# Moving a fourth expert from the loop into the fixed group, with the third weight matrix read in 8 KB runs

## The reference, cut to what matters

```python
def swiglu(h, w1, w3, w2):
    return (jax.nn.silu(h @ w1) * (h @ w3)) @ w2
...
    logits = (xt @ w_router).astype(jnp.float32)
    top_logits, top_idx = lax.top_k(logits, TOP_K)
    gates = jax.nn.softmax(top_logits, axis=-1)
...
    def expert_block(args):
        x_blk, e = args
        return swiglu(x_blk, w1[e], w3[e], w2[e])
```

## Time and profile before

| | |
|---|---|
| median of 3 runs | 1801.97 us (1798.7 to 1804.3) |
| the profiled execution | 1791.78 us, span 1790.1 us |
| up to the experts | 706 us |
| job 0 | 706 to 842 us |
| group, 168 slots | 842 to 1399 us |
| loop, three passes of 42 slots | 1399 to 1772.7 us |
| PE busy over the span | 94% |

### The profile page before, as it was taken

How to read it: one execution, slowest core, us unless ns; L and a number is a source line. 1 busy time by engine, 2 the same in 40 slices (tenths; PEclk the granted TensorE clock), 3 DMA queues, 4 the chain that set the end, 5 groups by cost and what they waited for, 6 DMA issues and landing times.

```text
span 1790.1 us, 23711 instructions
## 1 busy us (share of the span) xinstructions
PE 1686.4 (94%) x8929; PEld 1396.9 (78%) x8929; DVE 1400.4 (78%) x1439; ACT 1011.1 (56%) x953; POOL 65.5 (4%) x85
## 2 busy tenths in 40 slices
PE   5999979999999898999999999999999899999996
PEld 5988869999898877778777777776777688788875
DVE  4887777888788765997688777877887788888877
ACT  1544533333454445675666666666666667767664
POOL 1000100000100011000000000000000010010120
PEclk9998999999999898999999999999999999999999
DMA  9455657888545564997898898988899899999993
GB/s 309 151 174 158 232 165 232 271 285 272 189 158 171 188 213 166 357 356 269 314 338 322 296 333 314 341 319 313 326 327 348 298 367 375 360 378 362 359 390 154
DMA packets 270282, 503.62 MB, mean 281 GB/s; under 512 B 12630, under 2 KB 113256, under 8 KB 270184
## 3 DMA queue, kind: packets, MB, share of 16 engines
q1 hardware_dynamic: 262736, 489.72, 78.0%
q0 software_dynamic: 3056, 11.01, 1.8%
q10 hardware_dynamic: 4392, 1.57, 0.4%
HBM read 493.36 MB, written 8.91 MB: 281 GB/s over the span
## 4 chain that ended last, share of the span: by engine, by line
issue 42%; PE 40%; DVE 9%; ACT 4%; POOL 2%; DVEq 1%; ACTq 1%; POOLq 1%; DMA 0%
PE ps L1883 10%; PE ps L1885 9%; PE ps L1884 9%; DVE lo_ring L1789 5%; PE ps L2212 4%; PE ps L2211 4%; DVE lo_ring L1535 2%; ACT stage_hi L1151 2%; PE ps L2338 2%; ACT stage_hi L1085 1%; DVE xn L1824 1%; POOL rstd L814 1%; PE ps L2175 1%; POOL y_back L878 0%; POOL rstd L805 0%
## 5 line engine op out<-in xcount | busy, mean ns | idle before, releaser
L1789 DVE TENSOR_TENSOR lo_ring<-weight_ring,stage_hi 128x2048 fp32r<-128x2048 f32 x168 | 379.1, 2288 | 88.8 <-ACT stage_hi L1151 88.3
L1535 DVE TENSOR_TENSOR lo_ring<-weight_ring,stage_hi 128x2048 fp32r<-128x2048 f32 x168 | 378.2, 2288 | 61.7 <-ACT stage_hi L1085 61.1
L1085 ACT CAST stage_hi<-weight_ring 128x2048 fp32r<-128x2048 f32 x168 | 314.2, 1912 | 61.8 <-DMA weight_ring<-in_moe_w_dram 56.6
L1151 ACT CAST stage_hi<-weight_ring 128x2048 fp32r<-128x2048 f32 x168 | 314.4, 1911 | 5.7 <-DMA weight_ring<-in_moe_w_dram 5.7
L1883 PE MATMUL ps<-h_hi,stage_hi 128*128 128x256 f32 x800 | 233.2, 292 | 8.1 <-DVE h_lo L1248 6.3
L1883 PE MATMUL ps<-stage_hi,xe_hi 128*128 128x512 f32 x560 | 227.3, 406 | 10.2 <-DVE lo_ring L1535 8.8
L1285 DVE TENSOR_TENSOR lo_ring<-weight_ring,stage_hi 128x2048 fp32r<-128x2048 f32 x81 | 184.9, 2292 | 64.7 <-ACT stage_hi L950 57.3
L1884 PE MATMUL ps<-h_lo,stage_hi 128*128 128x256 f32 x800 | 229.6, 287 | 0.0
L1885 PE MATMUL ps<-h_hi,lo_ring 128*128 128x256 f32 x800 | 229.4, 287 | 0.0
L1884 PE MATMUL ps<-lo_ring,xe_hi 128*128 128x512 f32 x560 | 221.3, 395 | 0.0
L1885 PE MATMUL ps<-stage_hi,xe_lo 128*128 128x512 f32 x560 | 221.2, 395 | 0.0
(11 more groups left out here) (379 smaller groups left out, 2565.5 us busy)
## 6 DMA issues: line engine op xcount, KB each, us to landing
weight_ring<-in_moe_w_dram SPq DMA_DIRECT2D x336, 1024.0 KB, 6.9
weight_ring<-in_w_mod_dram SPq DMA_DIRECT2D x48, 1024.0 KB, 6.1
weight_ring<-in_w_in_dram SPq DMA_DIRECT2D x36, 1024.0 KB, 5.5
weight_ring<-in_ffn_w_dram SPq DMA_DIRECT2D x33, 1024.0 KB, 5.7
weight_ring<-in_w_out_dram SPq DMA_DIRECT2D x12, 1024.0 KB, 5.0
moe_rows<-y_moe POOLq DMA_DIRECT2D x5, 512.0 KB, 4.8
moe_rows<-y_e POOLq DMA_DIRECT2D x4, 512.0 KB, 8.2
x_tok<-in_x_dram SPq DMA_DIRECT2D x1, 1024.0 KB, 10.9
```

Source lines behind the costliest of these rows:

```text
L1085: nc.scalar.copy(jst_hi[i % JSTAGES][:], ring[:, n % RING, :]).then_inc(hi_ready, 1)
L1151: nc.scalar.copy(jst_hi[g % JSTAGES][:], ring[:, n % RING, :]).then_inc(hi_ready, 1)
L1535: nc.vector.tensor_tensor(ring_lo[:, n % RING, :], ring[:, n % RING, :], raw(jst_hi[i % JSTAGES][:]), ALU.subtract).then_inc(lo_ready, 1)
L1789: nc.vector.tensor_tensor(ring_lo[:, n % RING, :], ring[:, n % RING, :], raw(jst_hi[g % JSTAGES][:]), ALU.subtract).then_inc(lo_ready, 1)
```

## The change

The fourth smallest expert goes from the loop into the group: the loop has two passes, the group 210 slots. `behind` gets two runs of six S slots in each middle chunk, and four such runs in the last one. The columns, row places and step lists follow. The ACT wait for the last `sum` is gone; the last S expert ends before the last B slot (half 1 of w2), which takes its two blocks in the other order; the number of passes is read before the group on ACT, PE and DVE; and in a loop pass ACT copies `y_e` after four casts and after PE's first slot, no longer after three casts. In w2 the partition p now holds rows 4p to 4p+3 of a chunk, so that a transfer has runs of 8 KB in place of two of 4 KB for each partition. To match, every transposition of an activation (job 0, group and loop) takes every fourth column of its input.

```diff
-EXTRA = 3
+EXTRA = 4
...
-NSMALL = 3
-LOOP_MIN, LOOP_MAX = 4, 4 + EXTRA
+NSMALL = 4
+NOTHER = NE - 2 - NSMALL
+LOOP_MIN, LOOP_MAX = 1 + NOTHER, 1 + NOTHER + EXTRA
...
-        behind = [3, 1 if ch == 0 else 3, 1, 5, 3, 3] if ch < NCH - 1 else [3, 3, 6, 6, 0, 2]
+        behind = [3, 1 if ch == 0 else 3, 6, 6, 3, 3] if ch < NCH - 1 else [6, 6, 6, 6, 2, 0]
...
+def lag(c):
+
+    return 1 if c == LAST_C else 2
+
+
+def half_order(ch):
+
+    return (1, 0) if ch == NCH - 1 else (0, 1)
...
-                    (s_at(PLACES_C), ("places", 0)), (AT["B", "w2", NCH - 1, 1], ("next", 0)),
-                    (sum_at(2), ("sum", 2)))
+                    (s_at(PLACES_C), ("places", 0)), (sum_at(NSMALL - 1), ("next", 0)),
+                    (G_SLOTS, ("sum", NSMALL - 1)))
...
-    w2_v = moe_w2[0].rearrange("e (t p) n -> e p t n", p=P)
+
+    w2_v = moe_w2[0].rearrange("e (c p t) n -> e p c (t n)", p=P, t=4)
...
-            return w2_v[bass.ds(e, 1), :, ch * 4 + half * 2:ch * 4 + half * 2 + 2, :].rearrange("e p t n -> (e p) t n")
+            return w2_v[bass.ds(e, 1), :, ch:ch + 1, half * 2 * D:(half + 1) * 2 * D].rearrange("e p c n -> (e p) c n")
...
-                    act.wait_ge(st_used, ahead(job) + ND)
+                split(3)
+                if not first:
+
+                    act.wait_ge(st_used, ahead(job) + (ND + 1))
                     act.wait_ge(y_free, job + 1)
                     nc.scalar.copy(y_e[:], pair(YB)).then_inc(ye_out, 1)
-                split(3)
...
-            act.wait_ge(ssum_done, NSMALL)
...
-                        last = nc.tensor.transpose(ps[:, TPB, k * P:(k + 1) * P], m_act[:, ch % 2, k * P:(k + 1) * P], ident[:])
+                        last = nc.tensor.transpose(ps[:, TPB, k * P:(k + 1) * P], m_act[:, ch % 2, :].rearrange("p (n t) -> p t n", t=4)[:, k, :], ident[:])
...
-                    for t in range(TT):
+                    for t in half_order(c) if h else range(TT):
...
-                                last = mm(ps[:, SUP, at:at + SMALL], part[:, k * P:(k + 1) * P], fold[:], start=True, stop=True)
+                                last = mm(ps[:, SUP, at:at + SMALL], part.rearrange("p (n t) -> p t n", t=4)[:, k, :], fold[:], start=True, stop=True)
```

More of the change, by code:

```diff
@@ L180, in sum_at @@
     return AT["S", "w2", NCH * j + NCH - 1, 1]
-PLACES_C = 16
+def lag(c):
+    return 1 if c == LAST_C else 2
+def half_order(ch):
+    return (1, 0) if ch == NCH - 1 else (0, 1)
+PLACES_C = 22
 CS, BS = range(NSMALL * NCH), range(NCH)
-GROUP_PE = steps_at(*[(s_at(c), ("sT", c)) for c in CS], *[(s_at(NCH * j - 1), ("rows", j)) for j in (1, 2)],
-                    *[(b_at(ch), ("bT", ch)) for ch in BS], *[(sum_at(j) + 3, ("sum", j)) for j in range(2)],
-                    (s_at(PLACES_C), ("places", 0)), (AT["B", "w2", NCH - 1, 1], ("next", 0)),
-                    (sum_at(2), ("sum", 2)))
+GROUP_PE = steps_at(*[(s_at(c), ("sT", c)) for c in CS], *[(s_at(NCH * j - 1), ("rows", j)) for j in range(1, NSMALL)],
+                    *[(b_at(ch), ("bT", ch)) for ch in BS], *[(sum_at(j) + 3, ("sum", j)) for j in range(NSMALL - 1)],
+                    (s_at(PLACES_C), ("places", 0)), (sum_at(NSMALL - 1), ("next", 0)),
+                    (G_SLOTS, ("sum", NSMALL - 1)))
@@ L189 @@
 GROUP_ACT = steps_at((2, ("y0", 0)),
                      *[(AT["S", "w1", c, 1] + 2, ("s1", c)) for c in CS], *[(AT["S", "w3", c, 1] + 2, ("s3", c)) for c in CS],
-                     *[(s_at(c) + 2, ("silu", c)) for c in CS], *[(s_at(NCH * j - 1) + 2, ("rows", j)) for j in (1, 2)],
-                     *[(s_at(c) + 3, ("hi", c)) for c in CS],
+                     *[(s_at(c) + lag(c), ("silu", c)) for c in CS], *[(s_at(NCH * j - 1) + 2, ("rows", j)) for j in range(1, NSMALL)],
+                     *[(s_at(c) + lag(c) + 1, ("hi", c)) for c in CS],
@@ L193 @@
                      *[(AT["B", "w1", ch, 1] + 2, ("bsilu", ch)) for ch in BS], *[(b_at(ch) + 2, ("bhi", ch)) for ch in BS],
[L194 to L197, removed]
+                     *[(sum_at(j) + 2, ("raw", j)) for j in range(NSMALL - 1)],
@@ L198 @@
+                     *[(sum_at(j) + 5, ("sum", j)) for j in range(NSMALL - 1)],
+                     (G_SLOTS, ("next", 0)), (G_SLOTS, ("raw", NSMALL - 1)))
+GROUP_DVE = steps_at(*[(s_at(c) + lag(c), ("act", c)) for c in CS], *[(s_at(NCH * j - 1) + 2, ("rows", j)) for j in range(1, NSMALL)],
+                     *[(s_at(c) + lag(c) + 1, ("lo", c)) for c in CS],
                      *[(AT["B", "w3", ch, 1] + 2, ("bact", ch)) for ch in BS], *[(b_at(ch) + 2, ("blo", ch)) for ch in BS],
@@ L518, in build @@
         posj, mskj, gatej = (m(n, [P, TT, NCOL + 1]) for n in ("posj", "mskj", "gatej"))
[L519 removed]
+        pose, gate = (m(n, [P, TT, NE]) for n in ("pose", "gate"))
+        gmsk = drow
         selT = m("selT", [P, TT, P])
         cnts, over, ranki, rank, far = (m(n, [P, NE]) for n in ("cnts", "over", "ranki", "rank", "far"))
[L522 to L523 removed]
+        key, place, cap, few, base, step1, step_few, step7 = (m(n, [P, NE]) for n in (
+            "key", "place", "cap", "few", "base", "step1", "step_few", "step7"))
         shift = m("shift", [P, NCOL])
@@ L826, in _ @@
                     serve_blocks(l, ("post_mix", "post_ffn")[i])
-            cleared = [(k * P, P) for k in [0] + list(range(COL_LOOP + 3, NCOL + 1))]
-            cleared += [((COL_SMALL + j + 1) * P + SMALL, P - SMALL) for j in range(2)]
+            cleared = [(k * P, P) for k in [0] + list(range(COL_LOOP + NOTHER, NCOL + 1))]
+            cleared += [((COL_SMALL + j + 1) * P + SMALL, P - SMALL) for j in range(NSMALL - 1)]
             pool.wait_ge(y_zero, 1)
@@ L846, in _ @@
             nc.gpsimd.drain().then_inc(y_free, 1)
-            for j in range(2):
+            for j in range(NSMALL - 1):
                 row = (COL_SMALL + j + 1) * P
@@ L1814, in _ @@
                     elif step == "bsum":
-                        for t in range(TT):
-                            if t == 0:
+                        for n_half, t in enumerate(half_order(c)):
+                            if n_half == 0:
                                 dve.wait_ge(b_done, c + 1)
@@ L2302, in _ @@
                                                (wh[:, k, s], wl[:, k, s]), kk == 0, kk == 3)
-                        if h and t == 0:
+                        if h and t == half_order(c)[0]:
                             last.then_inc(b_done, 1)
```

36 lines of the change are left out of this document (18 added, 18 removed).

## The result

The changed kernel takes **1861.43 us** (median of 4 runs, 1858.69 to 1868.34) against 1802.93 for the kernel before on the same chip (4 runs): ratio 1.0339 [1.0322, 1.0355], **slower**. I had forecast 1787, faster. The profiled execution took 1861.65.

What follows compares the result with a forecast made beforehand. PE was taken to bound the kernel, with the DMA engines nearly full. The terms -122.6 + 95.0 + 16 - 4 gave -15.6, say -15 us, from the 1801.97 median to 1787 us; range 1770 to 1845.

Steps and rivals of the forecast that it cites:

- every fourth column: Fold and transposition loads stepping 16 bytes: taken as nothing; doubled loads bounded at 47.5 us for folds, 13.9 for transpositions.
- Rival 1: Fold and transposition loads by fourths are slow: full price +61 us, 1848 us, also visible in job 0; chance 0.27.
- the fold block: Sign in the group's folds: 16 take 1.7 us if skipping loads cost nothing, about 3.4 if they are slow.
- What leaves: Loop: the middle one of three passes goes, -122.6 us.
- What comes in: Group: a fourth small expert's matmuls, folds, row gather and final sum, +95.0 us.
- Waits of the new order: Group: PE waits in added runs of six S slots, behind ACT's copy and cast and DVE's subtraction, +16 us.
- The passage: Group to loop: PE starts the loop 4.9 us after its last group matmul, 2.9 less; with clock effect -4 us.
- Runs of 8 KB: w2 transfers: half as many packets, hidden under PE's matmuls, worth nothing; up to the +16 of waits if slots come early.
- Rivals 2 and 3: Group held by its slots, 3.32 us each: 1815 us, chance 0.11; earlier slots close waits: 1770 to 1759 us, chance 0.12.
- the sum: Whole kernel: -122.6 + 95.0 + 16 - 4 = -15.6 us.

Runs made afterwards that it cites:

- four only: Changed kernel with contiguous transpositions and the old w2 transfer runs, keeping the fourth small expert, order and passage; 1794.91 us, ratio 0.9942 to the kernel before.
- the wait back: The four only version with ACT's old wait for the last sum restored in front of the loop; 1793.72 us, ratio 0.996 to the kernel before.
- the contiguous version: Changed kernel keeping its 8 KB layout, but reading contiguous columns, so w2 meets wrong columns; 1796.65 us, ratio 0.9966 to the kernel before.
- pairs: Changed kernel with two w2 rows per partition, still 8 KB runs, transpositions taking every second column (8 bytes); 1796.73 us, ratio 0.9958 to the kernel before.
- fourths only: Kernel before with only the 8 KB w2 transfers and every-fourth-column transpositions added, three small experts; 1852.76 us, ratio 1.0282 to the kernel before.
- half by fourths: Changed kernel with the first 8 folds of each block stepping by four columns, the other 8 contiguous; 1819.55 us, ratio 1.0081 to the kernel before.
- four steps: Changed kernel with contiguous transpositions and folds stepping 4, 8, 12 or 16 bytes by chunk, taking wrong columns; 1821.54 us, one run.

## Why the prediction was wrong

**The step that failed** is the one headed *every fourth column*: "I take nothing, by the nearest row". The row was a moving operand that comes in at 0.45 ns a column, and I concluded that a load at 0.9 was not at the limit of the memory. That row reads *contiguous* columns, so it says nothing of a read that skips, and the forecast had said itself that no row shows one. The folds measured +51.2 us, a little above the upper bound of 47.5, since a fold by fourths takes 0.221 us and not twice 0.106. The transpositions, bounded at 13.9, cost some 1 us: a block of eight takes 0.87 us where it takes 0.79 with four only (and the earlier trace rows shows 0.79 for eight others, of the gathered rows), although their loads grew from 141 to 207 ns. Their pace is not that of their loads, contrary to what I took. Rival 1 (chance 0.27, 1848 us) was the right mechanism, with the fold block as the sign that was named for it. That its 1848 lies near 1861 is in part luck: it holds 13.9 for transpositions that cost some 1, and nothing for the clock. Job 0, where it was to show too, has transpositions but no folds and is only 0.8 us longer.

**What no case held** is the clock. Against four only, 20.3 us of excess and 4.3 in the gathers, 24.6 in all, come from stretches at 1.2 GHz behind the slower blocks; without them the time would be some 1837, inside the range. I had priced the doubling of a load as added time only, and not asked what PE's doing less work in that time does to the clock; the first pass in the earlier trace rows, with 0.98 behind an idle stretch, was a hint that the clock answers to that.

**What held.**
- *What leaves*: -122.6 for a pass; the loop is 124.4 shorter, the difference being its faster first pass (124.73 against 125.40) and last pass (124.56 against 125.70).
- *What comes in*: +95.0; 77.8, 12.0, 3.5 and 1.9 make 95.2.
- *Waits of the new order*: +16; the waits before the S matmuls rose from 13.9 to 30.2, +16.3, the idle time in all by 17.4. That those of 1.12 us hang on ACT's copy of the w1 product is shown by moving the copy; for those of 1.3 us it is argued only, since they stayed.
- *The passage*: 4.9 us forecast from the last group matmul to the loop, 4.9 measured (the row at 1588.16 plus one distance, to 1593.27), against 7.8 before. Putting the wait back brings 1.7 us of it in the trace; the remainder goes with the last slot being a B slot, which was not tried alone.
- *Runs of 8 KB*: nothing, as forecast, by the contiguous version. Rivals 2 and 3 are out with it: the group of 42 more slots is 673 us at contiguous reads, not 557 + 139 - 3 = 693, and the waits did not close.

Left alone, the fourth expert and the passage give -8.7 us where the sum said -15.6. In the traces its expert part is 5.6 shorter: the loop gives 122.1, and the group and job 0 take 116.5, 8 more than 95 + 16 less the 2.9 of the passage. 3.5 of that stands in the ledger as low clock (5.7 less 2.2), about half of it one stretch behind the first fold block, which the version with the wait back does not have; 2.8 are idle time (18.8 for 16), and the rest are restarts too small to place.

## What to carry to other kernels

A layout that buys longer transfers pays on the side of the engine that reads it: count what the consumer's step in bytes becomes before counting the packets, and if no row of a trace shows such a read, hold the chance of the doubling much higher than the nearest contiguous row suggests. If a weight load must skip, a step of 8 bytes cost 0.09 us in a block of 16, one of 16 bytes 1.83. And where PE waits for DVE and DVE for ACT, look at which small step ACT has in front of the cast: one cast of delay in two of them was worth more here (24 us) than the whole move of an expert (9 us).

## What was not expected of the hardware

- Weight loads of 128 float32 columns with a step of 4, 8, 12 and 16 bytes let a fold start every 0.106, 0.113, 0.166 and 0.221 us. The transpositions' loads already grew from 141 to 206 ns at 8 bytes (pairs) and stayed at 207 at 16, at nearly the same pace. Why the two kinds differ is open.
- Blocks of 16 slow loads in 3.53 us were followed by matmuls at 1.2 GHz in 14 of 28 cases, in 8 of 21 (fourths only) and in 6 of 7 (four steps); blocks of 2.55 us (half by fourths), of 2.65 us (a step of 12 bytes) and of 32 fast loads in 3.49 us in none but the first of the group. Why it is 14 and not 28 is open.
